# Announcing far jumps earlier, and twice, in a mixture-of-experts stage

## The reference

```python
for e in range(N_EXPERTS):          # 16 experts, D_EXPERT = 1024
    hid = jax.nn.silu(t @ w_gate[e]) * (t @ w_up[e])
    y = y + combine[:, e:e + 1] * (hid @ w_down[e])
```

## Time and profile before

| what | us |
|---|---|
| median of 3 runs | 1766.48 (1765.78 to 1767.99) |
| the profiled execution, its time | 1769.38 |
| its span in the trace | 1767.7 |
| matmuls busy | 1510.8 (85% of the span) |
| weights and other bytes moved | 629.55 MB |
| experts, from the first gather to the last down unit | about 781 to 1750 of the span |

### The profile page before, as it was taken

How to read it: one execution, slowest core, us unless ns; L and a number is a source line. 1 busy time by engine, 2 the same in 40 slices (tenths; PEclk the granted TensorE clock), 3 DMA queues, 4 the chain that set the end, 5 groups by cost and what they waited for, 6 DMA issues and landing times.

```text
span 1767.7 us, 27610 instructions
## 1 busy us (share of the span) xinstructions
PE 1510.8 (85%) x12032; PEld 1000.0 (57%) x12032; DVE 584.6 (33%) x1095; ACT 188.8 (11%) x456; POOL 362.5 (21%) x161
## 2 busy tenths in 40 slices
PE   7799999999999999986699955798976666898558
PEld 6588788888888878653444522433433324335223
DVE  0453557877576243431111211113011110212013
ACT  0001012200001100041100100100101001001002
POOL 0005630187677877300000000000000000000000
PEclk9899999999999999988899988898998778899889
DMA  9997896588778654549997899998999999999996
GB/s 386 424 425 218 347 386 263 236 335 353 315 313 351 285 208 179 233 164 427 428 410 280 333 425 427 425 427 356 386 426 426 425 428 426 419 416 414 427 425 266
DMA packets 50926, 629.55 MB, mean 356 GB/s; under 512 B 5763, under 2 KB 8228, under 8 KB 11840
## 3 DMA queue, kind: packets, MB, share of 16 engines
q1 hardware_dynamic: 49192, 621.32, 85.0%
q10 hardware_dynamic: 1560, 5.80, 0.8%
HBM read 623.43 MB, written 3.67 MB: 355 GB/s over the span
## 4 chain that ended last, share of the span: by engine, by line
PE 63%; DMA 31%; issue 2%; DVE 2%; POOL 1%; SPq 1%; ACT 0%; DVEq 0%; ACTq 0%; POOLq 0%
PE bank L1635 23%; PE bank L925 14%; DMA ring<-in_w_up_gate 10%; DMA ring<-in_w_down 9%; PE bank L1397 8%; PE bank L954 6%; DMA region_g<-in_w_up_gate 5%; PE bank L1473 4%; DMA region_g<-in_w_down 4%; DMA ring<-in_ada_w 2%; PE bank L888 2%; PE bank L966 2%; DMA ring<-in_w_in 1%; POOL ring L773 1%; PE bank L961 1%
## 5 line engine op out<-in xcount | busy, mean ns | idle before, releaser
L773 POOL TENSOR_TENSOR ring<-ring 128x1024 f32<-128x1024 f32 x152 | 360.0, 2396 | 329.4 <-DMA ring<-in_w_in 226.7
L925 PE MATMUL bank<-ring,region_b 128*32 128x256 f32 (+1 forms) x3104 | 305.5, 477 | 120.3 <-DMA ring<-in_w_up_gate 94.5
L925 PEld LDWEIGHTS bank<-ring,region_b 128*32 128x32 f32 (+1 forms) x3104 | 129.1, 129 | 278.9 <-issue 142.6
L954 PE MATMUL bank<-ring,region_f 128*32 128x256 f32 (+1 forms) x1920 | 171.0, 449 | 56.3 <-DMA ring<-in_w_down 56.2
L1635 PE MATMUL bank<-ring,region_a 128*128 128x256 f32 x768 | 171.4, 380 | 2.7 <-DVE region_e L2406 2.2
L1635 PE MATMUL bank<-ring,region_x 128*128 128x256 f32 x768 | 170.4, 379 | 0.9 <-issue 0.8
L1635 PEld LDWEIGHTS bank<-ring,region_a 128*128 128x128 f32 x768 | 145.3, 190 | 25.5 <-issue 5.2
L1635 PEld LDWEIGHTS bank<-ring,region_x 128*128 128x128 f32 x768 | 145.3, 190 | 21.1 <-issue 1.1
L954 PEld LDWEIGHTS bank<-ring,region_f 128*32 128x32 f32 (+1 forms) x1920 | 71.2, 122 | 140.8 <-issue 63.8
L2721 DVE TENSOR_TENSOR work<-work,bank 128x128 f32<-128x128 f32 (+1 forms) x32 | 10.3, 321 | 423.1 <-ACT work L1900 423.1
L2208 DVE SCALAR_TENSOR_TENSOR bank<-ring,condT,bank 128x512 f32<-128x512 f32 x192 | 144.8, 754 | 5.8
(11 more groups left out here) (262 smaller groups left out, 1299.9 us busy)
## 6 DMA issues: line engine op xcount, KB each, us to landing
ring<-in_w_up_gate SPq DMA_DIRECT2D x111, 2048.0 KB, 29.5
ring<-in_w_down SPq DMA_DIRECT2D x56, 2048.0 KB, 20.8
ring<-in_ada_w SPq DMA_DIRECT2D x44, 2048.0 KB, 11.8
ring<-in_w_in SPq DMA_DIRECT2D x31, 2048.0 KB, 14.0
region_g<-in_w_up_gate SPq DMA_DIRECT2D x16, 2048.0 KB, 26.1
ring<-in_w_branch SPq DMA_DIRECT2D x8, 2048.0 KB, 14.6
ring<-in_w_out SPq DMA_DIRECT2D x8, 2048.0 KB, 10.5
region_g<-in_w_down SPq DMA_DIRECT2D x8, 2048.0 KB, 30.5
```

The costliest lines, as they stand in the source:

```text
L773: ins = pool.tensor_tensor(quarter(s, *out)[:, k:k + 4, :], quarter(s, *in0)[:, k:k + 4, :], quarter(s, *in1)[:, k:k + 4, :], op)
L925: last = nc.tensor.matmul(bank_of(x, j)[n * c:n * c + n, 0:2 * m], tokens(x, 8 * half + k), w[:, k % 4, :, m * c:m * c + m], start=(half = ...
L954: last = nc.tensor.matmul(bank_of(x, q)[n * c:n * c + n, 0:m], hidT[x][:, k, :], w[:, k % 4, m * c:m * c + m], start=(k == 0), stop=(k == ...
```

## The change

Four edits, all in PE's program. (1) `small_begin`, and with it the first part of a wide body, also multiplies the second half of unit 0. A narrow body, which holds both parts in one, keeps its order. (2) `woven_begin` does so too; `woven_units` then multiplies the first half of unit 1 where the second half of unit 0 stood, between gather and turn, and nothing stands between the turn and the wait for "tokens" but the turn of the weights. (3) A large body announces its jump back ahead of the first down unit. (4) At the same place it announces the next expert's question as well. Code that stands behind shifts by the instructions added.

```diff
@@ ask_once
             if announced is not None:
                 jump.branch_hint(announced)
+            question[name] = jump
@@ woven_begin
                 gate_up(0, 0, 0, first)
+                loaded_half(0, 1)
+                gate_up(0, 0, 0, last)
@@ woven_units
                 for x in xs:
                     extra("gather")(x)
-                loaded_half(0, 1)
-                gate_up(0, 0, 0, last)
+                loaded_half(1, 0)
+                gate_up(0, 0, 1, first)
                 for x in xs:
                     extra("turn")(x)
                 turn_weights()
-                loaded_half(1, 0)
-                gate_up(0, 0, 1, first)
                 for x in xs:
                     extra("tokens")(x)
@@ small_begin
                 gate_up(base, 0, 0, first).then_inc(half_used, 1)
+                loaded_half(0, 1)
+                gathered((1,))
+                gate_up(base, 0, 0, last).then_inc(half_used, 1)
@@ units
                 else:
-                    loaded_half(0, 1)
-                    gathered((1,))
-                    gate_up(base, 0, 0, last).then_inc(half_used, 1)
                     gathered((2, 3))
@@ expert_pe, ahead of the first down unit
             if base == NARROW and ne < NE - 1:
                 large_announced[pe, ne + 1] = pe.mark_branch_hint_location()
+            announced = pe.mark_branch_hint_location() if base == WIDE else None
+            if base == WIDE and ne < NE - 1:
+                question[f"pe{(ne + 1) // GRP}_{(ne + 1) % GRP}"].branch_hint(pe.mark_branch_hint_location())
@@ expert_pe, between the down units
-            announced = pe.mark_branch_hint_location() if base == WIDE else None
```

More of the change, by code:

```diff
@@ L860, in program @@
         large_announced = {}
+        question = {}
         def leave(eng, label, announced):
```

## The result

The changed kernel takes 1797.16 us (1796.07 to 1797.93), 30.7 us more than before; the ratio is 1.017, 95% interval 1.0157 to 1.0184. The prediction had 1780.5 and a range to 1785: slower, as it said, by twice the amount. The profiled execution spans 1796.2 us against 1767.7, so there are 28.5 us to account for.

The account below looks back on a forecast made before the run. The weight stream bounds the expert stage, except where full places make it wait for PE. Turn 3 6.8, turn 7 -0.6, turn 8 0.1 and turn 13 7.7 sum to 14.0 us: 1766.5 to 1780.5, range 1762.5 to 1785.

Parts of the forecast that it names:

- the notes: In large bodies, the question's announcement overwrites the jump back's, so the jumps back miss; chance 0.74.
- The miss of 5.2 us: At each jump back, one whole fetch on demand, taken as 5.2 us within 2.9 to 6.6.
- the clock's 1.7: After a missed jump back, PE's first 32 matmuls run at the lower clock, 1.7 us more.
- the three points that pass lateness on: First halves of turns 3, 7 and 13: PE's loss or gain there moves the whole weight stream behind.
- 5.2 less 2.0: At turn 7, the missed jump back loses 5.2 us; its correctly announced question saves 2.0.
- the first parts: Longer first parts: turn 2 gains 0.1 us, turn 6 gains 3.8, turn 12 loses 1.1.
- It takes 3.6, to 1152.2, and hides the fetch: In turn 6's first part, the second half's 3.6 us of matmuls cover L853's fetch of up to 6.6 us.
- PE has caught up by more than a half: At turn 8, entry may miss but PE has slack: 0 to 1.5 us late, taken as 0.1.
- some 2 us of it: In turn 3, the untaken question's announcement delays the next block some 2 us, behind the point that matters.

Follow-up runs that it names:

- order swapped: The changed kernel with its two announcements in the other order, question first and jump back second: ratio 1.0048, +8.5 us against the kernel before.
- early alone: The kernel before with only the jump back's announcement moved ahead of the first down unit: ratio 1.0001, +0.2 us.
- both early: The kernel before with jump back and then question announced ahead of the first down unit, first parts as before: ratio 1.0133, +23.5 us.
- turn 7's not announced: The kernel before with only the wide bodies' jump back, turn 7's alone in this run, left unannounced: ratio 1.0006, +1.1 us.

## Why the prediction was right or wrong

**Right: the notes.** "A fetcher that looks one block ahead and was never seen to take two suggests one note, which the second overwrites": shown by order swapped, early alone and both early. The order that I read from the code was the one in the trace (948.1 and 948.2 in turn 2). The miss of 5.2 us was 5.34 to 6.38, the clock's 1.7 is there (32 matmuls of turns 8 and 13 in 3.64 instead of 1.93), and the three points that pass lateness on are those of rows 2. One term came out for another reason than I gave. The idle time ahead of turn 7 grew by 1.94 us (9.80 for 7.86) where I had 5.2 less 2.0: the miss cost 6.04 and the shorter question gave back 4.05, but the kernel with no jump back announced has 2.5 of these without any announcement of the question.

**Wrong: the first parts (from a turn's first matmul to its extra tiles: turn 2 +4.0 for -0.1, turn 6 -0.7 for -3.8, turn 12 +4.3 for +1.1).** The step that failed was "It takes 3.6, to 1152.2, and hides the fetch (L853 took up to 6.6 us, from 1144.2)". I moved the matmuls and left the branch at its place in time. It stands behind them in PE's program, and behind the wait for the second half, so its 6 us move too. In turn 2 the gather waits 2.10 us for 1.00 and, after this, runs at the lower clock: 32 in 5.34 for 3.64. Sum of the three: 7.6 us against -2.8, so some 10 of the 16.7 us between forecast and measurement. By the measured times the first parts cost 6.2 us alone, and 8.5 with the code at the changed kernel's addresses, where the forecast had a gain of 2.8.

**Wrong: turn 8 (7.1 us for 0.1).** The second step that failed was "PE has caught up by more than a half; from 0 to 1.5 us, I take 0.1". I priced only turn 8's entry, found slack for it, and there was (turn 7's not announced, +1.1 us). I had noted for turn 3 that a wrong announcement delays the next block, and put it at nothing in turn 8, where it comes behind the first 32 matmuls and on top of a miss: 7.42 us of idle time instead of 3.59. In turn 3, where I had expected some 2 us of it, there was none.

**Not counted: the layout.** One instruction more in each large body, and the moved halves, shift the far code. The first parts alone cost 6.2 us at one place, 20.3 at another; the kernel before itself 6.0. The range had nothing for it. So a part of each experiment's few microseconds may be such a shift, and a difference under 0.4% between two of them says nothing by itself.

## What to carry to other kernels

The fetch for a far branch that isn't announced in time starts when the sequencer gets to the branch. Work put ahead of it to cover the fetch therefore delays the fetch, most of all if that work waits for data. Before the change the branch was reached 0.1 us into 3.6 us of matmuls; that is the cover to look for, or bring the target into the block at hand (0.22 us). Count announcements as one register: the last one stands. A wrong one can cost some 6 us, as the code in line then comes late, though it did not in every turn. Before pricing what an announcement gives, look at the same branch in a kernel without it. Before believing a change of a few microseconds in a program with far jumps, shift its code with nothing else changed and see how much that alone moves.

## What the runs showed of the hardware

- One announcement stands at a time and the last one counts: with the jump back's first and the question's second all jumps back take 5.3 to 6.4 us, with the order swapped 0.31 to 0.42 us, and then turn 7's question takes 6.5 us as if not announced. Up to three edges of blocks, counted in the compiled program, may lie between announcement and jump without loss (jump back early: 0.32 to 0.35 us).
- A jump back to code that isn't there took 5.1 to 7.7 us. Turn 7's question took 6.5 to 7.2 us behind a jump back that hit when it was not announced, or not last; 5.1 when announced last, just ahead of the jump; and 2.6 to 4.1 behind a jump back that missed, announced or not.
- A wrong announcement can make the next block late (7.4 to 7.7 us of idle time in turn 8 instead of 1.2 with the same miss), and did not in turns 3 and 13 of the changed kernel. Why, is open.
- A target once fetched isn't lost when the announcement is replaced (0.33 to 0.44 us with the question announced last).
- An announcement of the jump to the body, some 35 or 68 instructions ahead of it, didn't shorten it (6.0 to 6.6 us without it, 5.9 to 6.9 with it), but in turn 12 of two kernels it took 2.01 and 3.63 us, and in turn 7 of two others 2.31 and 4.48. Why there, is open.
- The same announced jump can hit or miss when only its code has moved, 5 us each time. Two kernels can differ at the same place in a block (turn 2's jump back, instruction 22: 5.13 and 0.42 us). No rule was found that fits all.
